# Four more page buffers for values in a one-core decoder step, filled while key pages are turned

## The reference, cut to what matters

```
k_past = cache_k[page_table]                       # 8 pages a request
means  = block sums of k_past / BLOCK              # 4 blocks of 256 tokens
idx    = top_k(q . means, 3)                       # per query and head
p      = softmax([q . k_selected - slope * dist, q . k_own - ...])
h      = p_selected @ v_selected + p_own @ v_own
x      = layer_norm(ALPHA * x + h @ w_out_b)
```

## Time and profile before

| | us |
|---|---|
| runs, median (lowest to highest) | 949.11 (947.41 to 958.73) |
| profiled execution, own time | 949.64 |
| its span, first to last instruction | 947.0 |
| TensorE busy | 920.5 (97%) |
| DVE, ACT, POOL busy | 629.2, 434.5, 56.3 |
| key pages turned | about 438 to 562 |
| value pages, first half | about 567 to 617 |
| value pages, second half | about 620 to 663 |

### The profile page before, as it was taken

The page is one execution under the profiler, slowest core; times in us unless marked ns, Lnnn a source line. Parts: engine busy times, 40 slices in busy tenths (PEclk is TensorE's granted clock), DMA queues, the critical chain, the costliest instruction groups (busy, mean ns, idle before and its releaser), DMA issues.

```text
span 947.0 us, 18965 instructions
## 1 busy us (share of the span) xinstructions
PE 920.5 (97%) x7594; PEld 857.4 (91%) x7594; DVE 629.2 (66%) x1116; ACT 434.5 (46%) x817; POOL 56.3 (6%) x69
## 2 busy tenths in 40 slices
PE   9999989999999999999999999989899999999996
PEld 8999877899999999998888779868799999999994
DVE  6576568768977475775676756434568797757555
ACT  5344654466445363544443552334547644536321
POOL 0000006400000000310000000000120000000000
PEclk9999999999999999999999999989899999999998
DMA  9962213744445445557887998998654545544301
GB/s 288 278 204 90 89 45 94 218 145 157 146 144 161 150 138 172 172 179 260 283 291 268 345 346 319 399 383 337 207 150 144 165 143 188 162 135 152 117 1 55
DMA packets 134224, 182.77 MB, mean 193 GB/s; under 512 B 5846, under 2 KB 116126, under 8 KB 134137
## 3 DMA queue, kind: packets, MB, share of 16 engines
q1 hardware_dynamic: 126142, 175.98, 56.4%
q10 hardware_dynamic: 7354, 3.49, 1.4%
q0 software_dynamic: 640, 2.10, 0.8%
HBM read 175.23 MB, written 6.32 MB: 192 GB/s over the span
## 4 chain that ended last, share of the span: by engine, by line
PE 92%; DVE 3%; ACT 2%; DMA 1%; issue 1%; ACTq 1%; SPq 0%; DVEq 0%; POOL 0%; POOLq 0%
PE ps L542 24%; PE ps L544 23%; PE ps L543 23%; PE ps L879 6%; PE ps L921 3%; PE ps L973 2%; DMA page<-in_cache_v_dram 1%; PE ps L557 1%; PE ps L575 1%; PE ps L958 1%; ACTq L1170 1%; PE ps L728 0%; PE ps L852 0%; ACT probs_turned L1354 0%; PE ps L641 0%
## 5 line engine op out<-in xcount | busy, mean ns | idle before, releaser
L1050 ACT ACTIVATE w_hi<-raw 128x1024 fp32r<-128x1024 f32 x192 | 202.6, 1057 | 256.8 <-PE ps L544 250.9
L1433 DVE TENSOR_TENSOR w_lo<-raw,w_hi 128x1024 fp32r<-128x1024 f32 x192 | 235.0, 1225 | 113.2 <-ACT w_hi L1050 112.9
L542 PE MATMUL ps<-x_hi,w_hi 128*128 128x322 f32 (+1 forms) x888 | 279.5, 315 | 0.0
L544 PE MATMUL ps<-x_hi,w_lo 128*128 128x322 f32 (+1 forms) x888 | 276.4, 311 | 0.0
L543 PE MATMUL ps<-x_lo,w_hi 128*128 128x322 f32 (+1 forms) x888 | 275.9, 311 | 0.0
L542 PE MATMUL ps<-h_hi,w_hi 128*128 128x320 f32 x640 | 200.1, 313 | 2.7 <-DVE h_lo L1571 1.7
L543 PE MATMUL ps<-h_lo,w_hi 128*128 128x320 f32 x640 | 198.3, 310 | 0.0
L544 PE MATMUL ps<-h_hi,w_lo 128*128 128x320 f32 x640 | 198.3, 310 | 0.0
L542 PEld LDWEIGHTS ps<-x_hi,w_hi 128*128 128x128 f32 x888 | 168.0, 189 | 5.4 <-ACT k_turned L1320 2.9
L543 PEld LDWEIGHTS ps<-x_lo,w_hi 128*128 128x128 f32 x888 | 168.5, 190 | 0.2
L544 PEld LDWEIGHTS ps<-x_hi,w_lo 128*128 128x128 f32 x888 | 167.5, 189 | 0.0
(11 more groups left out here) (345 smaller groups left out, 894.2 us busy)
## 6 DMA issues: line engine op xcount, KB each, us to landing
raw<-in_w_up_dram SPq DMA_DIRECT2D x32, 1024.0 KB, 5.7
raw<-in_w_down_dram SPq DMA_DIRECT2D x32, 1024.0 KB, 5.2
page<-in_cache_k_dram SPq DMA_DIRECT2D x64, 512.0 KB, 5.4
page<-in_cache_v_dram SPq DMA_DIRECT2D x64, 512.0 KB, 6.4
raw<-in_w_in_a_dram SPq DMA_DIRECT2D x12, 1024.0 KB, 9.1
raw<-in_w_kv_dram SPq DMA_DIRECT2D x8, 1024.0 KB, 7.2
raw<-in_w_out_a_dram SPq DMA_DIRECT2D x4, 1024.0 KB, 5.3
raw<-in_w_q_b_dram SPq DMA_DIRECT2D x4, 1024.0 KB, 5.3
```

The lines of the kernel that those rows point to most:

```text
L542: mm(out, WH[t % SPL][:, k, :], hi[:, k, 0:width], start=(k == 0), stop=False)
L544: last = mm(out, WL[t % SPL][:, k, :], hi[:, k, 0:width], start=False, stop=(k == 7))
L1050: A(WH[t % SPL][:, :, :], raw[RBUF[u]][:, :, 128 * (t % 2):128 * (t % 2) + 128], ACT.Copy)\
L1433: V.tensor_tensor(WL[t % SPL][:, :, :], raw[RBUF[t // 2]][:, :, 128 * (t % 2):128 * (t % 2) + 128], WH[t % SPL][:, :, :].bitcast(F32), ALU ...
```

## The change

Four page buffers are added (8 to 11), each of 4 KB a partition: the fourth place of `w_hi`, the fourth place of `w_lo`, the memory of the squares and row sums (`FS`, `A1`, `A2`, used by layer norms), and the padded queries `QZ[0]`. For that, tiles of the key and value projections use three places (`PLACE`) instead of four. Value pages 0 to 3 go into the new buffers while keys are turned: after key pages 13, 20, 29 and 36, the last one after a wait for 16 scored pairs. From then on value pages take turns in twelve buffers, from value page 50 on in ten (the two weight places are left out). Splits run one tile less ahead from the end of the query projection to the end of the value projection. The output projection's tiles 0 and 1 are split in prompt steps 4 and 5, tiles 2 and 3 after the value pages, tile 3 when the pages in the weight places have been read. Weight units stand 4 to 10 pages later in SP's queue.

```diff
+PLACE = [(t - 8 * Q_WK) % 3 if Q_WK <= t // 8 <= Q_WV else t % SPL for t in range(NT)]
+PLACE_BEFORE = [max((w for w in range(t) if PLACE[w] == PLACE[t]), default=-1) for t in range(NT)]
+EARLY, LEFT_OUT = 4, 50
+PAGE_AT = [g % RING for g in range(NPG)]
+_turn = [RING + i for i in range(EARLY)] + list(range(RING))
+for _v in range(NPG):
+    if _v == LEFT_OUT:
+        _turn = [b for b in _turn if not RING <= b < RING + 2]
+    PAGE_AT.append(_turn[0])
+    _turn = _turn[1:] + _turn[:1]
...
-                if g >= RING:
-                    sp.wait_ge(s_used, g - RING + 1)
-                sp.dma_start(page[g % RING][:, :], cache[bass.ds(number, 1)].rearrange("a t h d -> (a t) (h d)"))\
-                    .then_inc(s_in[g % RING], 16)
+                if PAGE_BEFORE[g] >= 0:
+                    sp.wait_ge(s_used, PAGE_BEFORE[g] + 1)
+                sp.dma_start(page[PAGE_AT[g]][:, :], cache[bass.ds(number, 1)].rearrange("a t h d -> (a t) (h d)"))\
+                    .then_inc(s_in[PAGE_AT[g]], 16)
...
             load_unit(4 * Q_WK + 2)
+            sp.wait_ge(s_mm, 8 * Q_WQ + 8)
+            pages(8, 14)
+            load_page(NPG)
+            pages(14, 18)
             load_unit(4 * Q_WK + 3)
-            pages(8, 22)
+            pages(18, 21)
+            load_page(NPG + 1)
+            pages(21, 26)
             load_unit(4 * Q_WV)
-            pages(22, 30)
+            pages(26, 30)
+            load_page(NPG + 2)
+            pages(30, 34)
             load_unit(4 * Q_WV + 1)
-            pages(30, 40)
+            pages(34, 37)
+            sp.wait_ge(s_sc, 16)
+            load_page(NPG + 3)
+            pages(37, 42)
             load_unit(4 * Q_WV + 2)
-            pages(40, NPG + 9)
+            pages(42, NPG)
+            pages(NPG + EARLY, NPG + 16)
             load_unit(4 * Q_WV + 3)
-            pages(NPG + 9, NPG + 19)
+            pages(NPG + 16, NPG + 25)
             load_unit(4 * Q_WOB)
-            pages(NPG + 19, NPG + 28)
+            pages(NPG + 25, NPG + 34)
             load_unit(4 * Q_WOB + 1)
-            pages(NPG + 28, 2 * NPG)
+            pages(NPG + 34, 2 * NPG)
...
-                split_to(t + 4)
+                split_to(min(t + 4, 8 * Q_WK + 2))
...
-                    split_to(8 * Q_WK + n + 3)
+                    split_to(8 * Q_WK + n + 2)
...
-                split_to(8 * Q_WV + n + 3)
+                split_to(min(8 * Q_WV + n + 2, 8 * Q_WV + 7))
...
                 p_step(i)
+                if i in (4, 5):
+                    split_to(8 * Q_WOB + i - 4)
...
+            split_to(8 * Q_WOB + 3)
```

More of the change, by code:

```diff
@@ L43 @@
 RAW, SPL = 4, 4
+PLACE = [(t - 8 * Q_WK) % 3 if Q_WK <= t // 8 <= Q_WV else t % SPL for t in range(NT)]
[8 more added lines that the diff above has]
+    _turn = _turn[1:] + _turn[:1]
+PAGE_BEFORE = [max((w for w in range(g) if PAGE_AT[w] == PAGE_AT[g]), default=-1) for g in range(2 * NPG)]
+PAGE_LOADS = [PAGE_AT[:g + 1].count(PAGE_AT[g]) for g in range(2 * NPG)]
+PLACES_FREE = max(g for g in range(2 * NPG) if RING <= PAGE_AT[g] < RING + 2) + 1
 K_FIRST = 2
@@ L156, in build @@
         raw = [put(f"raw{i}", [128, 8, 256]) for i in range(RAW)]
+        wh_at = [at[0] + 3 * 4096]
         WH = [put(f"w_hi{i}", [128, 8, 128], F32R) for i in range(SPL)]
+        wl_at = [at[0] + 3 * 4096]
         WL = [put(f"w_lo{i}", [128, 8, 128], F32R) for i in range(SPL)]
@@ L246, in build @@
         raw_at = [raw2_at]
-        page = [put(f"page{i}", [128, DM], F32, w_) for i, w_ in enumerate([b_] * 4 + [raw_at] * 4)]
+        sq_at = [fs_at]
+        page = [put(f"page{i}", [128, DM], F32, w_)
+                for i, w_ in enumerate([b_] * 4 + [raw_at] * 4 + [wh_at, wl_at, sq_at])]
         var = put("ln_var", [128, T], F32, lt_at)
@@ L275, in build @@
         evc, vc, rsc, nmr = [fin[:, i, :] for i in range(4)]
+        qz_at = [b_[0]]
+        page.append(put("page11", [128, DM], F32, qz_at))
         QZ = [put("q_padded0", [128, H, 4, 32], F32, b_)]
@@ L341, in build @@
             sem(n) for n in ("pS_done", "p_max", "p_exp", "p_norm", "p_turn", "p_turn_copied", "p_out", "p_out_copied")]
-        s_in = [sem(f"page_in{i}") for i in range(RING)]
+        s_in = [sem(f"page_in{i}") for i in range(RING + EARLY)]
         s_used, s_half = sem("page_used"), sem("page_half_turned")
@@ L541, in dense @@
                         pe.wait_ge(*chunk_ready(k))
-                    mm(out, WH[t % SPL][:, k, :], hi[:, k, 0:width], start=(k == 0), stop=False)
-                    mm(out, WH[t % SPL][:, k, :], lo[:, k, 0:width], start=False, stop=False)
-                    last = mm(out, WL[t % SPL][:, k, :], hi[:, k, 0:width], start=False, stop=(k == 7))
+                    mm(out, WH[PLACE[t]][:, k, :], hi[:, k, 0:width], start=(k == 0), stop=False)
+                    mm(out, WH[PLACE[t]][:, k, :], lo[:, k, 0:width], start=False, stop=False)
+                    last = mm(out, WL[PLACE[t]][:, k, :], hi[:, k, 0:width], start=False, stop=(k == 7))
                 last.then_inc(s_mm, 1)
@@ L879, in turn_page @@
                         last = nc.tensor.transpose(bank[:, 128 * j:128 * j + 128],
-                                                   page[P % RING][:, 128 * h:128 * h + 128], ident)
+                                                   page[PAGE_AT[P]][:, 128 * h:128 * h + 128], ident)
                     last.then_inc((s_half, s_used)[half], 1)
@@ L974, in page_values @@
                                   PT[G][:, 8 * a_ + p, 32 * j:32 * j + 32],
-                                  page[g % RING][:, 128 * h:128 * h + 128],
+                                  page[PAGE_AT[g]][:, 128 * h:128 * h + 128],
                                   start=(bb % 2 == 0 and p == 0 and a_ == 0), stop=True, skip_group_check=True)
@@ L1047, in split @@
                     act.wait_ge(s_raw[RBUF[u]], 16 * RUSE[u])
-                if t >= SPL:
-                    act.wait_ge(s_mm, t - SPL + 1)
-                A(WH[t % SPL][:, :, :], raw[RBUF[u]][:, :, 128 * (t % 2):128 * (t % 2) + 128], ACT.Copy)\
+                if PLACE_BEFORE[t] >= 0:
+                    act.wait_ge(s_mm, PLACE_BEFORE[t] + 1)
+                if t == 8 * Q_WOB + 3:
+                    act.wait_ge(s_used, PLACES_FREE)
+                A(WH[PLACE[t]][:, :, :], raw[RBUF[u]][:, :, 128 * (t % 2):128 * (t % 2) + 128], ACT.Copy)\
                     .then_inc(s_hi, 1)
```

8 lines of the change are left out of this document (4 added, 4 removed).

## The result

The changed kernel is slower: 959.52 us, median of 20 runs (956.71 to 963.34), against 949.83 (947.05 to 958.73) for the kernel before in as many runs beside it. The ratio is 1.0088, 95% interval 1.0069 to 1.0107, so the loss is 8.4 us (6.6 to 10.2), within the 2% called no change. The forecast was 949.3 with a range up to 952.5: too low. The profiled execution took 957.56, its span is 955.8, against 947.0 before: +8.8 us.

The account below looks back on a forecast made before the run. The prediction took TensorE as the bound (92% of the chain), time being lost or won only where it stands still. Its terms, -1.2 + 1.4 = +0.2 us, gave 949.3 us, range 945.0 to 952.5.

Parts of the forecast that it names:

- The moved weight units: SP's load queue: units behind 4 to 10 more pages are still loaded a whole tile ahead of need, 0 us.
- the 2.3 us for the prompt weights: First prompt step: TensorE's wait for the first normalised prompt weights shifts but keeps its 2.3 us.
- The rival of the clock: TensorE after 626.70: its clock stays up with fewer stops, 3.4 us faster, 945.9; chance 0.2.
- Term 1: Value page 28: four pages on chip earlier remove TensorE's page wait, -1.2 us.
- Term 2: Prompt steps 4 and 5: the splits moved there delay ACT, DVE and TensorE, +1.4 us, bounds 0 and 4.6.
- the rival to which I gave 0.1: Prompt steps: DVE's idle 2.30 us takes up the moved splits, so only the page wait shows, 947.9; chance 0.1.
- The fourth page: Key stage: the fourth early value page, with the burst behind it, makes no key page late, 0 us.
- the upper bound: Key stage, fourth early value page: 1.5 us if each of the ten loads takes 1.48 us.
- Early pages 0 to 2: Key stage: three early value pages fit in free DMA time, hidden under key pages, 0 us.
- The rule on 358 GB/s: HBM loads, about 358 GB/s per core: set aside for the trace's 410; by it the sum carries some 1.5 us more.
- The range: Whole kernel: the median was to lie from 945.0 to 952.5 us.
- TensorE works on tiles 0 and 1 there for over 7 us at its lower clock: Start of the output projection: this work hides the later splits of tiles 2 and 3, 0 us.

Follow-up runs that it names:

- the stores late: ACT's three stores of new values moved from ahead of the first prompt step to behind the last: changed kernel 947.86 us, kernel before 947.69 us.
- one unit later: Kernel before with the output projection's second weight unit behind value page 33, not 27, and tile 2 split after the value pages: 956.57 us, ratio 1.0087.
- eight pages ahead: Changed kernel where, from value page 30 on, SP waits until the page eight places ahead has been read: 956.41 us, ratio 1.0062.
- both repairs: Changed kernel with ACT's three stores behind the prompt steps and the fourth early value page behind key page 51: 944.84 us, ratio 0.9934.
- the later fourth page: Changed kernel with the fourth early value page moved from behind key page 36 to behind key page 51: 956.05 us, ratio 1.0059.

## Why the prediction was wrong, point by point

- **"The moved weight units ... are each needed a round or more later ...: 0".** This step failed. I asked who needs each unit and not what else is in the DMA engines when it goes by. The price of moving the second one of the output projection, alone in the kernel before, is a ratio of 1.0087, some 8 us (1.4 of them may be the gap of the last section): ACT's last two stores take 9.79 us to issue and not 4.78, TensorE waits 7.3 and not 2.3, and its clock is low for longer. Two things stay open: by what the unit lengthens the issue, and how much of the changed kernel's 8 us is the unit's and how much the twelve buffers', since moving it alone there didn't give them back.
- **"Once the wait is gone, the next thing TensorE meets is the 2.3 us for the prompt weights, which shifts with it and stays."** It became 9.1. The 4.78 us of the earlier trace rows looked like a cost of ACT's queue; it was a cost that depends on the traffic beside it (1.3 us for the third store with no loads, 10.94 with loads all along). A look at the DMA queues at 623 would have shown that the stores ran in a hole; the sum had no term for what becomes of it when a load is added ahead of it. The rival of the clock had the right place with the wrong sign: it had fewer pages outstanding.
- **Term 1, -1.2.** Right: the wait is gone, pages 0 to 28 are 1.4 us shorter. Page 28 is issued at 598.98, lands 8.8 us later and is used at 611.2, a lead of 3.4 us where 3.8 were forecast. Whether it can be had with the units in their old places no run tests.
- **Term 2, +1.4 for the moved splits.** Too high. In the changed kernel the waits for `p_turned` grew by 0.5; with the stores late they are 0.5 in both kernels, and in step 1 or in steps 4 and 5 the splits give the same time. The gap of 1.1 to 1.3 us inside step 6 isn't theirs either: the kernel before with one unit later has it (1.4) without a split in any prompt step. So DVE's idle 2.30 us can take them up, the rival to which I gave 0.1.
- **The fourth page, 0 "by 0.7 us only".** Too low: 1.5 us of waits, as much as the upper bound. That bound was itself off: ten loads at 1.48 us and not 1.28 are 2.0 us, less the 0.7 in hand 1.3. And the mechanism was another: not each page was slower but one page and the unit, and page 42 waited 1.38 us, page 43 only 0.17. The forecast named the point from which it decides, 1.36 us a page; the burst took 1.41 on average. With the stores late, moving it later took the ratio from 0.9976 to 0.9934, which is 4 us; the waits that went are 1.7, the two intervals overlap, and more than these waits isn't shown.
- **Early pages 0 to 2: 0.** Right, no wait in the key stage belongs to them.
- **The rule on 358 GB/s** (the Trainium skill, "DMA: Bandwidth & Descriptors", section "Where 436 GB/s comes from"): I set it aside for windows of 410 and 381 GB/s. In the burst the rate was 372, above it but nearer to it than to 410, and the 1.5 us more that I set beside it are what the waits came to, in part by luck, as the point on the fourth page says. My mistake was to take the densest window of another stage for the rate of this one. As a limit it still doesn't hold: 407 GB/s over 15 us in the changed kernel with late stores.
- **The range** took in no case above 952.5, because the stores of new values had no bound of their own: their 4.78 us came from one row, at one traffic, and could only shrink.
- **A reading.** "TensorE works on tiles 0 and 1 there for over 7 us at its lower clock": the low clock ends some 4 us into them, at 672.6. It changes nothing in the sum.

## What to carry to other kernels

A load that is early enough for its user can still be in the way: before moving one, list what is issued by other engines in the next ten to twenty us, above all stores in small packets, and see whether they run in a gap of the load queue. Keep stores off an engine that stands in a chain TensorE waits for, or issue them where that engine has nothing due; here moving the stores was worth 10.6 us in the changed kernel, the four buffers some 4 at best. And when a row shows an issue of several us, read the DMA queues of that window before carrying the row to another kernel as a constant.

## What the runs showed of the hardware that I had not expected

**Packets share, not bytes.** 788 packets of 512 bytes against 780 of some 4 KB in 8 us, and 819 against 766 in the kernel before over the same 8 us. The Trainium skill, "DMA: Bandwidth & Descriptors", section "Queues, rings and completion order", says that each DMA engine goes round the queues that have work, packet by packet, and that a packet holds some 9 to 17 descriptors. The trace agrees with the turns; what it counts as packets alternates one for one. The same page, section "Issuing engines are not separate DMA queues", says that starting a DMA usually takes little time beside the DMA itself. Here it took 10.94 us for a 0.25 MB store and held all of ACT's work.

**What ends a blocked issue** isn't settled. When the third store's issue ended, 799 packets of the stores were done in the changed kernel, 1,028 before, 1,448 with the one unit moved, and 248 with the stores late (4.7 us of issue). So it is no plain count of packets over all 16 DMA engines. The trace has one event for each engine's end of the first store: 624.5 to 628.8 in the kernel before, 626.6 to 631.7 with the one unit moved. The engines differ by up to 5 us, and one that is behind might hold the issue; with the stores late that doesn't fit without more, and no run tests it.

**The spread of the kernel before.** Its 35 runs beside the first experiments lay between 945.7 and 957.0; with the stores late, 12 runs beside them lay between 944.6 and 950.1. The four of the 35 above 956 have a mean granted clock of 0.980 to 0.985, as the kernels with the long wait do, the four fastest 0.989 to 0.992. That would fit a long issue in some executions and not in others; only one execution can be seen, so it isn't shown.

**A gap in TensorE without a wait.** Nine of the fourteen traces show it inside one matmul of two passes; timeline of the changed kernel with late stores:

```profile
647.54 0.27 PE L892 MATMUL ps<-p_turned,v_tok 128*128 128x128 f32 x1
649.07 0.27 PE L892 MATMUL ps<-p_turned,v_tok 128*128 128x128 f32 x1 [1.26 <-issue]
```

A 16 KB packet of the queue named instruction ended at 647.6, 1.4 us before that matmul (1.3 to 1.5 in the nine). With eight pages ahead the packet ended at 656.3 and the matmul came at 657.73, with both repairs 646.9 and 648.27, with one unit moved in the kernel before 659.6 and 660.91, with the later fourth page 658.4 and 659.86 (a gap of 0.23). In the changed kernel it ended at 658.0, before that matmul was due, and there is no gap. So I read it as a late load of code, up to 1.6 us; no run tested it. The Trainium skill, "Runtime: NRT & Kernel Launch", section "Instruction fetch mechanics", says that code comes in blocks of 16 KB and that the cost is mostly hidden; here it isn't always.
